# First block's mixer: in the gate and projection units the rounded weights meet operand and rest in one 512-column product, and the halves are added on VectorE

## What is computed

```python
for l in range(DEPTH):                      # first block, DEPTH = 2
    x = x + 0.5 * rmsnorm(swiglu(rmsnorm(x, ...), w_gu, w_down), ...)
    h = rmsnorm(x, mix_norm_pre[l])
    z = h @ w_in[l]
    aq, ak, av, mq, mk, mv, mo, mi, mf, gl = jnp.split(z, SPLIT_IDX, axis=-1)
    ya = diff_attention(aq, ak, av, lam, lam_init, attn_norm_w[l])
    ...                                     # convolution, mlstm_chunkwise -> hm
    ym = jax.nn.sigmoid(mo) * rmsnorm(hm, mlstm_norm_w[l])
    g_a, g_m = jnp.split(jax.nn.sigmoid(gl + gate_b[l]), 2, axis=-1)
    merged = g_a * (ya @ w_proj_a[l]) + g_m * (ym @ w_proj_m[l])
    x = x + rmsnorm(merged @ w_out[l], mix_norm_post[l])
    ...                                     # second feed-forward
```

## Time and profile before

| | |
|---|---|
| median of 3 runs | 1957.45 us (1957.35 to 1958.13) |
| the profiled execution: its own time | 1958.44 us |
| its span, first to last instruction | 1955.8 us |
| TensorE busy | 1941.7 us, 99% of the span |
| VectorE busy | 1269.5 us, 65% |
| ScalarE busy | 1099.4 us, 56% |
| granted TensorE clock, mean | 0.998 of full speed (2.4 GHz) |
| DMA, mean | 172 GB/s |
| gate and projection units of both layers | 64 of 624 |

### The profile page before, as it was taken

One profiled execution on the slowest core, in us unless ns is written; L12 is line 12 of the kernel. 1 busy time (PEld: TensorE's weight loads), 2 busy tenths in 40 slices (PEclk: granted clock), 3 DMA queues, 4 the chain that ended last, 5 costly groups with the idle time before them and its releaser, 6 DMA issues.

```text
span 1955.8 us, 29401 instructions
## 1 busy us (share of the span) xinstructions
PE 1941.7 (99%) x11580; PEld 1706.1 (87%) x11580; DVE 1269.5 (65%) x2141; ACT 1099.4 (56%) x1717; POOL 6.5 (0%) x18
## 2 busy tenths in 40 slices
PE   9999999999999999999999999999999999999998
PEld 7888899999788888888989988888989998989997
DVE  5555777466655575557865676556758777758775
ACT  5444666554644564456774655446656556646554
POOL 0000000000000000000000000000000000000000
PEclk9999999999999999999999999999999999999999
DMA  8656445546566556645454546664536555536562
GB/s 278 192 184 184 161 132 171 162 131 197 187 190 186 172 184 193 185 156 175 134 179 152 155 158 217 188 184 146 166 108 205 181 186 165 160 114 199 179 187 82
DMA packets 93688, 335.82 MB, mean 172 GB/s; under 512 B 10224, under 2 KB 12528, under 8 KB 93552
## 3 DMA queue, kind: packets, MB, share of 16 engines
q1 hardware_dynamic: 92112, 328.51, 54.0%
q0 software_dynamic: 720, 4.37, 0.6%
q10 hardware_dynamic: 720, 1.07, 0.2%
HBM read 332.86 MB, written 1.05 MB: 171 GB/s over the span
## 4 chain that ended last, share of the span: by engine, by line
PE 94%; DVE 4%; ACT 1%; DMA 1%; issue 1%; DVEq 0%; ACTq 0%
PE stream L1797 11%; PE stream L1798 10%; PE stream L1799 10%; PE stream L1803 10%; PE stream L1805 10%; PE stream L1804 10%; PE acc L1803 8%; PE acc L1805 8%; PE acc L1804 8%; PE stream L1897 1%; DVE w_lo L1061 1%; PE acc L2208 1%; PE acc L2006 1%; DMA w_raw<-in_w_down 1%; PE stream L2203 0%
## 5 line engine op out<-in xcount | busy, mean ns | idle before, releaser
L1061 DVE TENSOR_TENSOR w_lo<-w_raw,w_hi 128x1024 fp32r<-128x1024 f32 x624 | 759.7, 1223 | 391.4 <-ACT w_hi L550 390.4
L550 ACT ACTIVATE w_hi<-w_raw 128x1024 fp32r<-128x1024 f32 x624 | 655.1, 1055 | 423.4 <-PE stream L1805 208.6
L1797 PE MATMUL stream<-h_hi,w_hi 128*128 128x256 f32 x1440 | 417.0, 290 | 1.1 <-DVE conv_tiles L1513 0.9
L1798 PE MATMUL stream<-h_lo,w_hi 128*128 128x256 f32 x1440 | 407.0, 283 | 0.0
L1799 PE MATMUL stream<-h_hi,w_lo 128*128 128x256 f32 x1440 | 407.0, 283 | 0.0
L1803 PE MATMUL stream<-w_hi,h_hi 128*128 128x512 f32 x896 | 353.9, 395 | 0.0
L1805 PE MATMUL stream<-w_lo,h_hi 128*128 128x512 f32 x896 | 349.2, 390 | 0.0
L1804 PE MATMUL stream<-w_hi,h_lo 128*128 128x512 f32 x896 | 348.8, 389 | 0.0
L1797 PEld LDWEIGHTS stream<-h_hi,w_hi 128*128 128x128 f32 x1440 | 275.4, 191 | 6.4 <-issue 2.4
L1798 PEld LDWEIGHTS stream<-h_lo,w_hi 128*128 128x128 f32 x1440 | 275.7, 191 | 0.9
L1799 PEld LDWEIGHTS stream<-h_hi,w_lo 128*128 128x128 f32 x1440 | 275.3, 191 | 0.0
(11 more groups left out here) (312 smaller groups left out, 2183.3 us busy)
## 6 DMA issues: line engine op xcount, KB each, us to landing
w_raw<-in_w_up SPq DMA_DIRECT2D x264, 512.0 KB, 3.7
w_raw<-in_w_mix SPq DMA_DIRECT2D x228, 512.0 KB, 3.6
w_raw<-in_w_down SPq DMA_DIRECT2D x132, 512.0 KB, 3.7
params<-in_params POOLq DMA_DIRECT2D x4, 859.5 KB, 5.7
out_x<-x_residual SPq DMA_DIRECT2D x4, 256.0 KB, 2.4
constants<-in_consts POOLq DMA_DIRECT2D x1, 832.0 KB, 7.6
x_residual<-in_x ACTq DMA_DIRECT2D x3, 256.0 KB, 7.1
x_residual<-in_x SPq DMA_DIRECT2D x1, 256.0 KB, 3.6
```

The source lines that it names most:

```text
L550: nc.scalar.activation(w_hi[:, u % RING], w_raw[:, u % RAW], ACT.Copy).then_inc(hi_ready, 1)
L1061: nc.vector.tensor_tensor(w_lo[:, u % RING], w_raw[:, u % RAW], w_hi[:, u % RING].bitcast(F32), ALU.subtract).then_inc(split_done, 1)
L1797: nc.tensor.matmul(dst, w_hi[:, s, w], hi, start=first, stop=False)
L1798: nc.tensor.matmul(dst, w_hi[:, s, w], lo, start=False, stop=False)
```

## The change

A second form of unit, `wide_unit`, serves units 48 to 79. The operand and its rest now lie side by side in one tile (`h_both`, `ya_both`, `ym_both`: 256 columns of the rounded operand, then 256 of the rest), so w_hi meets both in one product of 512 columns that fills a whole bank; w_lo meets the rounded operand in one product of 256 columns that goes to the first half. A unit is then 8 x (512 + 256) columns in 16 products instead of 8 x (256 + 256 + 256) in 24.

The bank's second half (w_hi times the rest) has to be added. ScalarE copies it out in its new step `rest` (L761 after) after the unit is done: to `gl` for the gate units, to one of two buffers `p_sum` (tile proj_sums) for the projection units. VectorE waits for that copy, adds the first half (L1453 or L1389 after), and then multiplies as before (L1456 or L1391 after). ScalarE's `rest(i)` stands at the end of its iteration i, before `hi_next` of iteration i + 1, and in units 72 to 79 before the rounding to h_hi. A few other lines only follow the new layout of the tiles.

```diff
--- before
+++ after
@@ -103,8 +103,8 @@
         h32, _ = sb("h32", [P, KT, T])
         y_sqr, _ = sb("y_squares", [P, QT, D], at=h32_at)
         mo_tok, _ = sb("out_gate_tok", [P, QT, D], at=h32_at)
-        h_hi, _ = sb("h_hi", [P, KT, T], F32R)
-        h_lo, _ = sb("h_lo", [P, KT, T], F32R)
+        h_both, _ = sb("h_both", [P, KT, 2 * T], F32R)
+        h_hi, h_lo = h_both[:, :, 0:T], h_both[:, :, T:2 * T]
         cst, _ = sb("constants", [P, NC])
         gn, _ = sb("gains", [P, NG])
         par, _ = sb("params", [P, NPAR])
@@ -135,13 +135,14 @@
         act_lo, _ = sb("act_lo", [P, NF, T], F32R)
         end_ffn = place[0]
         place[0] = region
-        ya_hi, _ = sb("ya_hi", [P, KT, T], F32R)
-        ya_lo, _ = sb("ya_lo", [P, KT, T], F32R)
+        ya_both, _ = sb("ya_both", [P, KT, 2 * T], F32R)
+        ya_hi, ya_lo = ya_both[:, :, 0:T], ya_both[:, :, T:2 * T]
+        p_sum, _ = sb("proj_sums", [P, 2, T])
         region2 = place[0]
         x_sq, _ = sb("square_sums", [P, T], at=region2)
         aqk, at = sb("attn_qk", [P, 2 * HEADS, T])
-        yms_hi, at = sb("ym_hi", [P, KT, T], F32R, at=region2)
-        yms_lo, _ = sb("ym_lo", [P, KT, T], F32R, at=at)
+        yms_both, _ = sb("ym_both", [P, KT, 2 * T], F32R, at=region2)
+        yms_hi, yms_lo = yms_both[:, :, 0:T], yms_both[:, :, T:2 * T]
         ym_at = place[0]
         av_tok, _ = sb("attn_v_tok", [P, QT, D])
         ym_tok, _ = sb("ym_tok", [P, QT, D], at=ym_at)
@@ -451,7 +453,10 @@
         YM_TURN = (57, 63, 65, 68)
 
         def out_bank(i):
-            return bank[i % 3 if i < U_MO else (i + 1) % 3][:, 0:T]
+            return out_wide(i)[:, 0:T]
+
+        def out_wide(i):
+            return bank[i % 3 if i < U_MO else (i + 1) % 3][:]
 
         V_FM, V_C1, V_OUT = 4, 14, 18
         FM_UNITS = 10
@@ -742,6 +747,18 @@
                     act.wait_ge(act_step, stepped())
                     nc.scalar.activation(m_rs[:, :, 0:z - a], m_rs[:, :, 0:z - a], ACT.Exp,
                                          scale=-0.5).then_inc(m_rstd, 1)
+
+                def rest(i):
+                    act.wait_ge(unit_done, u0 + i + 1)
+                    if i < U_PA:
+                        dst = gl[:, i - U_GL]
+                    else:
+                        dst, m = p_sum[:, i % 2], i - U_PA - 2
+                        if m >= 8:
+                            act.wait_ge(proj_done, l * 24 + 8 + 2 * (m - 8) + 1)
+                        elif m >= 0:
+                            act.wait_ge(proj_done, l * 24 + m + 1)
+                    nc.scalar.activation(dst, out_wide(i)[:, T:2 * T], ACT.Copy).then_inc(rest_taken, 1)
 
                 def ym_round(p):
                     act.wait_ge(ym_turned, l * 4 + p + 1)
@@ -812,6 +829,8 @@
                             act.wait_ge(gl_scaled, l * 16 + m + 1)
                             nc.scalar.activation(gl[:, m], gl[:, m], ACT.Sigmoid,
                                                  bias=p1("gate_b", m)).then_inc(gl_sig, 1)
+                    if i >= U_GL:
+                        rest(i)
                     if i == 70:
                         exp_set()
                     if i >= U_PM:
@@ -1366,8 +1385,10 @@
                 def proj(i):
                     m = i - U_PA
                     dve.wait_ge(gl_sig, l * 16 + m + 1)
-                    dve.wait_ge(unit_done, u0 + i + 1)
-                    nc.vector.tensor_tensor(gl[:, m], gl[:, m], out_bank(i), ALU.mult).then_inc(proj_done, 1)
+                    dve.wait_ge(rest_taken, l * 32 + i - U_GL + 1)
+                    nc.vector.tensor_tensor(p_sum[:, i % 2], p_sum[:, i % 2], out_bank(i), ALU.add).then_inc(dve_step, 1)
+                    dve.wait_ge(dve_step, stepped())
+                    nc.vector.tensor_tensor(gl[:, m], gl[:, m], p_sum[:, i % 2], ALU.mult).then_inc(proj_done, 1)
                     if i >= U_PM:
                         m = i - U_PM
                         dve.wait_ge(proj_done, l * 24 + 8 + 2 * m + 1)
@@ -1428,8 +1449,11 @@
                     if i in YM_TURN:
                         ym_rest(YM_TURN.index(i))
                     if U_GL <= i < U_PA:
-                        dve.wait_ge(unit_done, u0 + i + 1)
-                        nc.vector.tensor_tensor(gl[:, i - U_GL], out_bank(i), rs_all[:, 0:T],
+                        dve.wait_ge(rest_taken, l * 32 + i - U_GL + 1)
+                        nc.vector.tensor_tensor(gl[:, i - U_GL], gl[:, i - U_GL], out_bank(i),
+                                                ALU.add).then_inc(dve_step, 1)
+                        dve.wait_ge(dve_step, stepped())
+                        nc.vector.tensor_tensor(gl[:, i - U_GL], gl[:, i - U_GL], rs_all[:, 0:T],
                                                 ALU.mult).then_inc(gl_scaled, 1)
                     if U_PA <= i:
                         proj(i)
@@ -1812,6 +1836,16 @@
                     if waits:
                         waits(k)
                     r = product(dst, u % RING, k, hi[:, k], lo[:, k], k == 0, k == KT - 1)
+                r.then_inc(unit_done, 1)
+
+            def wide_unit(dst, u, both, waits=None):
+                for k in range(KT):
+                    if waits:
+                        waits(k)
+                    w = slice(k * P, (k + 1) * P)
+                    nc.tensor.matmul(dst, w_hi[:, u % RING, w], both[:, k], start=(k == 0), stop=False)
+                    r = nc.tensor.matmul(dst[:, 0:T], w_lo[:, u % RING, w], both[:, k, 0:T], start=False,
+                                         stop=(k == KT - 1))
                 r.then_inc(unit_done, 1)
 
             def turn(n, t):
@@ -2161,13 +2195,15 @@
                             chunk(c, j, t)
                         continue
                     waits(i)
-                    if i < U_PA:
+                    if i < U_GL:
                         model_unit(out_bank(i), u, h_hi, h_lo)
+                    elif i < U_PA:
+                        wide_unit(out_wide(i), u, h_both)
                     elif i < U_PM:
-                        model_unit(out_bank(i), u, ya_hi, ya_lo,
+                        wide_unit(out_wide(i), u, ya_both,
                                    (lambda k: pe.wait_ge(ya_split, l * 4 + 2 * (k // 4) + 2)) if i == U_PA else None)
                     else:
-                        model_unit(out_bank(i), u, yms_hi, yms_lo,
+                        wide_unit(out_wide(i), u, yms_both,
                                    (lambda k: pe.wait_ge(ym_split, n8 + k + 1)) if i == U_PM else None)
 
                 def merged(u):
```

7 lines of the change are left out of this document (4 added, 3 removed).

## The result

The changed kernel takes **1961.05 us** (median of 12 runs, 1960.24 to 1963.27) against 1957.69 us for the kernel before (12 runs, 1956.83 to 1958.84) on the same chip: ratio 1.0017, 95% interval 1.0010 to 1.0025. That is 3.4 us or 0.17% slower, just inside the 3.9 us (0.2%) that I called no change. The forecast was 1958.8 us with a range of 1955.0 to 1963.0. In a second session (experiment *again*) the same kernel gave 1.0023 (1.0014 to 1.0031), 4.4 us, just outside. So it is a small loss, and about 2 to 3 us above what my terms sum to.

The account below looks back on a forecast made before the run. TensorE, busy 1941.7 of 1955.8 us, was taken as the bound. Saving -6.8 plus waits of 3.2, 3.6 and 1.3 gave +1.3 us: 1958.8 us against the median 1957.45, range 1955.0 to 1963.0.

Parts of the forecast that it names:

- saving of 512 wide products: TensorE, units 48 to 79: each wide product saves 13.3 ns, 0.107 us per unit, 6.8 us less in all.
- values of heads 4 and 7: TensorE waits for mlstm_p before the values of these heads: 0.81 us, four times over both layers, 3.2 us.
- units 67 and 68: TensorE waits for banks freed by late gate multiplications: 0.99 and 0.82 us per layer, 3.6 us in both layers.
- unit 79: TensorE waits for its bank because VectorE and ScalarE's turns slow down: 0.66 us, 1.3 us in both layers.
- the turn at the mixer's end: ScalarE's last w_hi is just in time for the squares: nothing taken; other bound 1.2 us late, 2.4 in both layers.
- nothing saved: Rival for the wide products: the pair keeps 360 ns, net +4.7 us, 1962.2 us, slower; chance 0.12.
- The three places: Where TensorE soon takes delayed results in each layer: values of heads 4 and 7, units 67 and 68, unit 79.
- The ring at 3.90 us: Units 73 to 79: VectorE and ScalarE take turns at 3.90 us with the addition, against 3.45 before.
- With the transfer's 3.7 us ... just in time. I take nothing: Mixer's end: transfer plus 1.06 for w_hi ends at 38.0, squares due at 38.1, so no wait counted.
- the late start at the end of the mixer is real: Rival: transfers asked for in one burst make ScalarE 1.2 us late per layer; net +3.7, 1961.2 us; chance 0.15.
- no waits at all: Rival: idle time on ScalarE and VectorE absorbs all added steps; net -6.8, 1950.6 us, faster; chance 0.08 including nearly none.
- Half the waits: Rival: ScalarE's copy finds a gap and only additions count; net -2.2, 1955.2 us, no measurable change; chance 0.15.

Follow-up runs that it names:

- e2_wide_only: Against the kernel before: wide products in units 48 to 79 without ScalarE's copies or VectorE's additions, second halves never added; 1953.8 us, ratio 0.9979.
- e11_after_moved: Changed kernel with the last weight rounding moved behind the first half's norm, its rest behind y_tok; 1962.92 us, ratio 1.0027 against the kernel before.
- e5_proj_a: Against the kernel before: wide only in units 64 to 71, the projection units of ya; 2.8 us more, ratio 1.0014.
- e8_late_more: Wide in units 48 to 62 and 69 to 74, VectorE's steps for gates 55 and 61 behind mlstm_p; 1958.28 us against 1957.82 for the kernel before.
- e3_price: Changed kernel with seven of eight pairs per unit again three 256-column products, all copies and additions kept; 5.2 us more than the kernel before, ratio 1.0028.
- e9_copies: Changed kernel without the additions: second halves copied out by ScalarE but not added; 3.4 us less than the kernel before, ratio 0.9985.

## Why the prediction came out as it did

The sum was +1.3 us, and the runs give +3.4 and +4.4. The time fell into the range, and "no change" held by a hair in one session and not in the other. In part this was luck: errors cancel. The saving came 2.6 us short; the waits, which are shorter when TensorE arrives later, came 1.3 to 1.6 us short; the end of the mixer and the next block's start, at nothing in the sum, cost about 2. Step by step, both layers together:

| step | forecast | measured | from |
|---|---|---|---|
| saving of 512 wide products | -6.8 | -4.2 | e2_wide_only |
| values of heads 4 and 7 | +3.2 | +2.6 | steps after less products only |
| units 67 and 68 | +3.6 | +2.8 | the same |
| unit 79 | +1.3 | +1.1, +1.4 | the same, two profiles |
| the turn at the mixer's end | 0, bound 2.4 | +0.6, +1.6 | unit 80 to the turn, two profiles |
| the feed-forward block's start | not named | +1.2, +0.5 | the turn to conv_tiles, two profiles |
| sum | +1.3 | +4.1, +4.7 | distances: +4.0, +4.0; runs: +3.4, +4.4 |

(The second profile had the faster pitch in both layers, 0.6 us more of saving than the products-only one.)

- **"The new pair costs 226.7 + 120.0 = 346.7 ns"** was mis-sized: exactly true of some units, 353 ns in others, and gate units behind value products save 0.04 us instead of 0.107. The bound on the other side ("nothing saved") was not reached. Both terms I took from rows of a single size; no row before showed the mixture, as the text said. The Trainium skill (TensorE: Matmul & The Clock Gate, section "Wait — 56ns, not 53.3ns?") has 2.5 ns per product above the columns' time, an estimate of 1.3 us for 512 products. The products alone gave 4.2, so here both that figure and my 13.3 ns miss, and the truth lies between.
- **The three places were right**, and so was "six times" and "four times". The chain of steps was nearly right too. At the heads, counted from the first product of unit 54 (head 7: unit 60, the same to 0.02 us in the differences):

| us after unit 54's first product | before | products only | copies, no additions | after |
|---|---|---|---|---|
| mlstm_p starts | 9.60 | 9.59 | 10.08 | 10.54 |
| first product of the values | 10.83 | 10.61 | 10.68 | 11.15 |
| unit 57 starts | 11.86 | 11.63 | 11.81 | 12.28 |

mlstm_p and the additions ahead of it after, on VectorE:

```profile
392.66 0.41 DVE L1453 TENSOR_TENSOR gates_merge<-gates_merge,stream 128x256 f32<-128x256 f32 x1
393.10 0.42 DVE L1456 TENSOR_TENSOR gates_merge<-gates_merge,mix_rstd 128x256 f32<-128x256 f32 x1
...
394.58 0.55 DVE L1335 SCALAR_TENSOR_TENSOR mlstm_p<-acc,decay 128x384 f32<-128x384 f32 x1
```

The copies put mlstm_p 0.49 us later where I had 2 x 0.30, the addition 0.46 where I had 0.45: 0.95 against 1.05. That copies alone cost a head only 0.17 us is the room of 0.69 us at work, not a copy that came free. The wait, 0.54 us for 0.81 (10.61 to 11.15), is shorter because of those 0.10 us, because TensorE comes only 0.22 us earlier and not 0.32 (the mis-sized saving), and because it takes mlstm_p 0.06 us after its end and not 0.13. Unit 57 then loses 0.11 us more, as the products on the values follow each other more slowly after the wait: the step is 0.64 longer in all. Units 67 and 68, 1.4 us for 1.8, fall short for the same reasons: the multiplication of unit 64 ends 0.85 us later, counted from unit 63, for 1.05.
- **The ring at 3.90 us** was right to the hundredth, from L1389 to L1389 after:

```profile
470.99 0.41 DVE L1389 TENSOR_TENSOR proj_sums<-proj_sums,stream 128x256 f32<-128x256 f32 x1
...
474.89 0.41 DVE L1389 TENSOR_TENSOR proj_sums<-proj_sums,stream 128x256 f32<-128x256 f32 x1
```

- **"With the transfer's 3.7 us ... just in time. I take nothing"** is the step that failed. The reckoning named the right rounding, the right order and even the moment: it has the transfer asked for 13.0 us after unit 80, and so it was. But it gave 0.1 us of room and then used the median over the whole program. Before the change the transfer at this place, the second of four asked for within 3.5 us, took 4.5 and 4.6 us in the two layers; with that row the same sum has the turn 0.7 us late in each layer, 1.4 us in all, where 0.6 and 1.6 were measured. In the eight layers listed with `e11_after_moved` it took 3.8 to 6.1 us: a margin of 0.1 us against such a spread is no margin. My rival "the late start at the end of the mixer is real" describes it, and had a chance of only 0.15.
- **The feed-forward block's start was named nowhere.** In the first layer of the changed kernel the turn was on time and the block still started 1.0 us late: its second w_down transfer took 6.8 us for 5.9, asked for at the same time. Why, I have not shown. A plain guess, that the units hand back their w_raw slots later and so crowd the transfers, does not fit: in `e5_proj_a` and `e8_late_more` the transfers in that window are asked for at the same moments as without the loss, up to this one and the one behind it, and they still take up to 1.7 us longer. In 23 of the 28 layers the transfer took 5.8 to 6.2 us, in five 6.8 to 7.6, and all five are in kernels with wide projection units.
- **The rivals**: no waits at all (-6.8) was never near. Half the waits (-2.2) needed a copy that delays nothing; the copies put mlstm_p 0.49 us later. Nothing saved (+4.7) fell with the products alone, though `e3_price`, which builds it, measured +5.2, of which the units' part is +4.3: given TensorE's times without the saving, the prices at the named places were sized right (steps of +0.42, +0.61 and +0.72 us for waits of 0.49, 0.66 and 0.71).

## What to carry to other kernels

Saving instructions on the busiest engine by giving more to engines that are idle 35 or 44% of the time pays only where their result isn't taken at once: find those places by the distance from delivery to use, and move the new steps behind what is waited for there, as with gates 55 and 61 (2.6 us). A chain that runs slower than the bound engine carries its lateness to the next stage, where weight transfers are then asked for late (here 13.0 for 8.95 us after unit 80). Cost it there with the row of the same transfer before, not the program's median, and treat any margin below the spread as a wait.

## What I had not expected of the hardware

- Alternating products of 512 and 256 columns run at one of two pitches, 346.7 or 353 ns a pair, at a granted clock of 1.00 (2.4 GHz) in both; which one a run of units gets can differ between executions of the same kernel (2.83 and 2.77 us a unit in the two layers of the first profile, 2.77 and 2.77 in the second). What decides it is not shown. Equal sizes showed one pitch each, 120.0 and 226.7 ns.
- A wait of TensorE cost 0.1 us more than its length at the heads: behind it the first two products on the values of head 4 start 0.21 us apart after the change and 0.22 us apart in `e9_copies`; before, without a wait, 0.11 us.
- A transfer of 512 KB at the same place of the program, asked for at the same moment to 0.1 us, took 3.8 to 6.1 us. A rounding in an in-order queue turned that into 0 to 2 us of TensorE's time, of which the busy shares show nothing.
